# Gathering the U rows and the V rows of 512 tokens apart, with TensorE summing four tokens' V rows in 32-column parts

## The chip, the core and the metric

The kernel runs on one core of one Trainium2 chip. The metric is the device time of one execution in microseconds. The engines are TensorE (PE), VectorE (DVE), ScalarE (ACT), GpSimd (POOL) and SyncE (SP), and 16 DMA engines move data between memory and the on-chip buffers.

## What is computed

Two transformer blocks over 512 tokens of 1024 values in float32: projections, attentions, a convolution, cross attentions, and in the first block a product-key layer with 16384 single-neuron experts. This last part is what the change touches:

```python
# hf: normed tokens, in chunks of 128; 8 heads, 16 experts per head
experts = ...                      # 128 indices per token, from two top-16 lists per head
g = softmax(top_s)
ue = peer_u[experts]               # per token 128 rows of 1024 floats
ve = peer_v[experts]               # per token 128 rows of 1024 floats
act = gelu(einsum('td,thkd->thk', hc, ue))
y = einsum('thk,thkd->td', g * act, ve)
x = x + y
```

That is 512 x 128 rows of U and as many of V, 4 KB each: 537 MB in all.

## The kernel before

The tokens lie in X as four tiles of 128 (partition = token). Tiles 0 and 1 are half 0, tiles 2 and 3 half 1. The program is a list of steps made by `Plan.steps` (from line 454): the first part runs half 0 through the first block (`first_a`), the last part runs half 1 through the second block (`second(1, False)`), and between them three step streams are woven by made-up costs (`weave`, line 85): `work` (half 1 through the first block, then half 0 through the second), `peers` (the experts of all four tiles) and `choices` (the top-16 lists, `choose`). Every engine then runs those steps of the list that concern it, in the order of the list, and waits on semaphores. In `work` nearly every projection is a `proj_T` or `proj_tok` step, planned at 3.4 each, with one 512 KB block of weights that SP loads into RING (6 entries).

An expert step `(t, c)` of `peers` handles the c-th expert of all 128 tokens of tile t, and 512 of them are planned at 3.1 (tiles 0 and 1) or 2.5 (tiles 2 and 3):

- POOL (line 2160) gathers 128 rows of 8 KB from `in_uv`, where the U and the V row of an expert stand side by side, into one of 8 slots of 1 MB in BIG. Partition p gets the row of token p. It waits until the slot's earlier user has been added.
- DVE (line 1943) multiplies the U half by the normed tokens and sums over 1024 values: one dot product per token, in column `k % 8` of `dots`.
- ACT (lines 1441, 1445, 1448) takes the gelu of that one column and scales it by the gate.
- One or two steps later the V half is added to the tokens. For 333 of the experts DVE does it (line 1923, X = V * gate + X). For the other 179 ACT first writes a diagonal matrix of the gates (line 1453), and TensorE multiplies it with the V half into PSUM banks 6 and 7 (lines 1176, 1177). `Plan.peers` picks these 179. After a tile DVE adds the banks to X (`total`, line 1933).

A float32 matmul is recorded as two MATMUL instructions, so an add by TensorE is four of them, of 512 columns each. In the trace, `BIG<-in_uv,BIG` is the gather, `CUSTOM_DVE_ANT_0` of line 1943 the dot product, and `L908`/`L909` the projections of `work`.

## Time and profile before

| | |
|---|---|
| median of 3 runs | 2927.49 us (2926.61 to 2928.93) |
| span of the profiled execution | 2927.4 us |
| own time of the profiled execution | not listed apart from its span; the span is 0.1 us under the median |
| PE busy | 2491.4 us (85%) |
| DVE busy | 1760.7 us (60%) |
| ACT busy | 1133.8 us (39%) |
| POOL busy | 676.9 us (23%) |
| moved by DMA | 838.64 MB, mean 286 GB/s |
| first gather issued, first and last dot product | 559.4 us, 567.2 us and 2306.1 us |

How to read it: busy is the union of an engine's instructions. A stretch is bound by an engine only where that engine's busy time is near the stretch's length, or by the DMA engines where their share is near 1. Half of the kernel's time and more lies between the first and the last expert, so the stretches between them are read one by one, 64 expert steps in each.

### The profile page before, as it was taken

Reading aid. Unit: us, or ns where it says so; the run is one execution under the profiler, and the core shown is the slowest. Engines: PE = TensorE matmul, PEld = TensorE weight load, DVE = VectorE, ACT = ScalarE, POOL = GpSimd, SP = SyncE. Lnnn points to the kernel's source line nnn. Section 1 sums busy time; section 2 is a strip of 40 time slices with the busy share of each in tenths; the row PEclk is TensorE's granted clock in tenths of the full one; section 3 lists DMA queues with packets and bytes.
Section 4 is the critical chain, followed back from the end, with each engine's and each line's share of the span. In section 5 each row is a group of like instructions: output and inputs, shape, how many; then the busy total and the mean of one; then the engine's idle time right before and its main releaser. Section 6 shows DMA issues by size and latency. Waiting matters only on the chain.

```text
span 2927.4 us, 29566 instructions
## 1 busy us (share of the span) xinstructions
PE 2491.4 (85%) x10118; PEld 1743.2 (60%) x10118; DVE 1760.7 (60%) x4222; ACT 1133.8 (39%) x2762; POOL 676.9 (23%) x566
## 2 busy tenths in 40 slices
PE   8999999879989759888968678588985799988998
PEld 7786666667755437546736544264763376655883
DVE  2101311598797778666989888878998416412430
ACT  2101301242533765354442578464554325512210
POOL 0000000122234343332223445444223101100000
PEclk9999999989989889999989578799997999999999
DMA  5545243689999999999899989999999743432443
GB/s 197 173 154 168 95 144 129 219 335 351 390 394 417 409 397 392 419 389 384 299 332 402 365 301 385 396 420 419 417 418 416 277 159 109 151 130 88 153 155 116
DMA packets 160966, 838.64 MB, mean 286 GB/s; under 512 B 17400, under 2 KB 21896, under 8 KB 95024
## 3 DMA queue, kind: packets, MB, share of 16 engines
q0 software_dynamic: 73728, 536.90, 45.8%
q1 hardware_dynamic: 82464, 287.75, 28.0%
q10 hardware_dynamic: 4624, 12.11, 1.1%
q8 instruction: 80, 1.31, 0.2%
q14 instruction: 70, 0.57, 0.1%
HBM read 828.27 MB, written 8.41 MB: 286 GB/s over the span
## 4 chain that ended last, share of the span: by engine, by line
PE 55%; DVE 18%; ACT 12%; DMA 11%; issue 4%; POOL 0%; ACTq 0%; DVEq 0%; SPq 0%
PE ps L908 26%; DMA BIG<-in_uv,BIG 10%; PE ps L928 5%; PE ps L929 5%; PE ps L1152 5%; DVE BIG L1943 5%; DVE X L1923 4%; PE ps L909 4%; PE ps L1176 2%; PE ps L1177 2%; ACT L1441 2%; DVE BIG L1854 1%; PE ps L1122 1%; DVE BIG L1851 1%; PE ps L1101 1%
## 5 line engine op out<-in xcount | busy, mean ns | idle before, releaser
L2160 POOL DMA_INDIRECT BIG<-in_uv,BIG x512 | 634.2, 1239 | 1646.3 <-DVE BIG L1900 564.6
L908 PE MATMUL ps<-BIG,RING 128*128 128x256 f32 x3472 | 807.6, 385 | 13.8 <-DMA RING<-in_w_cq 4.9
L908 PEld LDWEIGHTS ps<-BIG,RING 128*128 128x128 f32 x3472 | 670.1, 194 | 133.4 <-issue 28.6
L1943 DVE CUSTOM_DVE_ANT_0 BIG<-BIG 128x1024 f32<-128x1024 f32 x512 | 619.6, 1217 | 85.4 <-DMA BIG<-in_uv,BIG 84.2
L1923 DVE SCALAR_TENSOR_TENSOR X<-BIG,small,X 128x1024 f32<-128x1024 f32 x333 | 426.6, 1281 | 91.7 <-ACT small L1445 91.6
L1441 ACT ACTIVATE small<-small 128x1 f32<-128x1 f32 x512 | 102.6, 200 | 620.7 <-DVE small L1943 619.4
L908 PE MATMUL ps<-WK,RING 128*128 128x256 f32 x1232 | 287.2, 385 | 25.2 <-DVE BIG L1702 23.2
L908 PEld LDWEIGHTS ps<-WK,RING 128*128 128x128 f32 x1232 | 235.7, 193 | 65.3 <-DVE BIG L1702 31.1
L928 PE MATMUL ps<-RING,BIG 128*128 128x512 f32 (+1 forms) x448 | 223.0, 579 | 5.0 <-DVE BIG L1681 2.4
L929 PE MATMUL ps<-RING,BIG 128*128 128x512 f32 (+1 forms) x448 | 222.6, 578 | 0.0
L1274 ACT ACTIVATE BIG<-ps 128x256 f32<-128x256 f32 (+2 forms) x143 | 56.8, 398 | 408.5 <-PE ps L909 343.2
L1640 DVE TENSOR_SCALAR BIG<-ps 128x256 f32<-128x256 f32 (+2 forms) x37 | 16.8, 454 | 255.8 <-PE ps L909 211.4
L1176 PE MATMUL ps<-BIG,DG 128*128 128x512 f32 x180 | 111.4, 704 | 66.8 <-ACT DG L1453 66.7
L1152 PE MATMUL ps<-RING,BIG 128*128 128x512 f32 x352 | 159.8, 608 | 1.5 <-DVE X L1933 1.5
L896 PE MATMUL ps<-ident,BIG 128*128 128x128 f32 x128 | 47.8, 386 | 131.0 <-ACT BIG L1245 76.2
L1441 ACT ACT_TABLE_LOAD x117 | 150.1, 1283 | 2.7 <-issue 0.6
L909 PE MATMUL ps<-BIG,RING 128*128 128x256 f32 x496 | 147.5, 379 | 0.0
L1633 DVE TENSOR_TENSOR X<-ps,X 128x512 f32<-128x512 f32 x40 | 27.5, 690 | 196.9 <-PE ps L929 116.5
L929 PEld LDWEIGHTS ps<-RING,BIG 128*128 128x128 f32 x448 | 85.1, 190 | 101.0 <-issue 99.5
L928 PEld LDWEIGHTS ps<-RING,BIG 128*128 128x128 f32 x448 | 84.4, 190 | 102.0 <-issue 92.6
L1176 PE MATMUL ps<-BIG 128*128 128x512 f32 x178 | 109.1, 699 | 37.3 <-ACT BIG L1453 37.1
L1223 ACT ACTIVATE WK<-X 128x1024 f32<-128x1024 f32 x32 | 33.8, 1055 | 222.2 <-DVE X L1633 207.2
(259 smaller groups left out, 3136.7 us busy)
## 6 DMA issues: line engine op xcount, KB each, us to landing
RING<-in_w_up SPq DMA_DIRECT2D x88, 512.0 KB, 6.0
RING<-in_w_down SPq DMA_DIRECT2D x66, 512.0 KB, 3.6
RING<-in_w_pq SPq DMA_DIRECT2D x32, 512.0 KB, 6.1
RING<-in_w_cc SPq DMA_DIRECT2D x16, 512.0 KB, 8.1
RING<-in_w_cx SPq DMA_DIRECT2D x16, 512.0 KB, 4.1
RING<-in_w_cb SPq DMA_DIRECT2D x16, 512.0 KB, 4.4
RING<-in_w_cv SPq DMA_DIRECT2D x16, 512.0 KB, 5.0
RING<-in_w_gc SPq DMA_DIRECT2D x16, 512.0 KB, 4.7
```

The costliest lines, as they stand in the source:

```text
L908: e.matmul(ps[:, 0:256], W[:, j, :], src[:, j, 0:256], start=j == 0, stop=False)
L909: e.matmul(ps[:, 0:256], W[:, 7, :], src[:, 7, 0:256], start=False, stop=True).then_inc(pe.sem, pe("mm", site, h, c, m))
L928: e.matmul(ps[:, 0:n], src[:, 2 * j, t * 128:(t + 1) * 128], W[:, 0, :], start=j == 0, stop=False)
L929: mm = e.matmul(ps[:, 0:n], src[:, 2 * j + 1, t * 128:(t + 1) * 128], W[:, 1, :], start=False, stop=j == 3)
L1152: mm = e.matmul(ps[:, :], AF[h][:, f, t * 128:(t + 1) * 128], W[:, hh * 512:(hh + 1) * 512], start=f == 0, stop=f == 21)
L1176: e.matmul(banks[6][:, :], d, v[:, 0:512], start=first, stop=last)
L1177: e.matmul(banks[7][:, :], d, v[:, 512:1024], start=first, stop=last).then_inc(pacc.sem, pacc("sum", k))
L1274: e.activation(dst, ps[:, 0:dst.shape[-1]], ACT.Copy, scale=scale).then_inc(act.sem, act("ev", site, h, c, m))
L1441: e.activation(a, dots[:, k % 8:k % 8 + 1], ACT.Gelu).then_inc(act.sem, act("gelu", k))
L1923: e.scalar_tensor_tensor(out=X[:, t, :], in0=slot[slot_of[k]][:, 1024:2048], scalar=acts[:, k % 8:k % 8 + 1], in1=X[:, t, :], op0=ALU.mult ...
L1943: e.tensor_tensor_reduce(out=u, in0=HF[:, t % 2, :], in1=u, scale=1.0, scalar=0.0, op0=ALU.mult, op1=ALU.add, accum_out=dots[:, k % 8:k % ...
L2160: e.indirect_dma_start(out=slot[i], out_offset=None, in_=I["uv"], in_offset=bass.IndirectOffsetOnAxis(ap=IDX[:, t, c:c + 1], axis=0)).then ...
```

## The change

U and V become two tensors. A step of `peers` is now a row step of 512 KB, U or V, and there are 1024 of them, planned at half of the former cost. The slots are 15 of 512 KB (13 while half 1's score lists borrow two). A V row step exists once all 128 U rows of its tile are in the plan, and goes ahead of any U row step; so the order is U of tile 0, V of tile 0, U of tile 1, and so on.

- U row step `(t, c)`: gather of the c-th expert's U rows for 128 tokens, then DVE's dot product into column c of `DOTS`, which also frees the slot.
- After the 128th U row of a tile: one gelu over 128x128 on ACT, one multiply with the gates on DVE, one transpose by TensorE and a copy (`GATES_T`: partition = expert, column = token). The indices are transposed in the same way after row 104.
- V row step `(t, n)`: gather of the 128 V rows of one token n, partition = expert.
- For every four tokens m, 32+m, 64+m, 96+m: DVE copies 4 gate columns into `SPREAD`, a buffer of zeros, and TensorE does 8 matmuls of a 128x32 stationary part with 512 columns, each into the 32 PSUM partitions that hold its token. All 32 such groups of a tile add up in banks 6 and 7.

DVE's 333 adds, ACT's 512 gelus and 512 scalings, its 179 diagonals and TensorE's 716 MATMUL records for the diagonals go. 512 further gathers, 128 groups of 8 matmuls (16 records each), 128 small copies and 4 chains of gelu, multiply, transpose and copy come. `second(0)` also waits in the plan for the total of tile 1.

```diff
     def take_slot(self, row):
+        lent = self.lent_from is not None and (3, 3) not in self.chosen
+        self.turn += 1
+        if self.turn >= (13 if lent else 15):
+            self.turn = 0
+        self.slot_of[row] = self.turn
...
+            u_ok = u < 512 and (tu, cu // 32) in self.chosen
+            v_ok = v < 512 and tv in summable
+            pace = 1.55 if min(tu, tv) < 2 else 1.25
+            if u_ok and not v_ok:
...
+                yield 0, "urow", tu, cu
+                if cu == 104:
+                    after(0, "turn_ids", tu)
+                if cu == 127:
+                    summable.add(tu)
+                    after(2, "gelu", tu)
+                    after(3, "weigh", tu)
+                    after(4, "turn_gates", tu)
+                yield pace, "pace"
+            elif v_ok:
...
+                yield 0, "vrow", tv, 32 * j + m
+                if j == 3:
+                    after(2, "spread", tv, m)
+                    after(3, "vsum", tv, m)
+                if iv == 127:
+                    after(7, "total", tv)
+                yield pace, "pace"
...
-        NS = 8
+        NS = 15
...
+            def vsum(t, m):
...
+                w.wait_ge(*at["spread", t, m])
+                for j in range(4):
+                    w.wait_ge(*at["slot", "v", t, 32 * j + m])
+                for hh in range(2):
+                    for j in range(4):
+                        d = spread_at(t, m) + 32 * j - m
+                        v = slot[slot_of["v", t, 32 * j + m]][:, hh * 512:(hh + 1) * 512]
+                        mm = e.matmul(banks[6 + hh][32 * j:32 * j + 32, :], SPREAD[:, d:d + 32], v, start=m == 0, stop=m == 31)
+                mm.then_inc(vsums.sem, vsums("vsum", t, m))
...
-                e.scalar_tensor_tensor(out=X[:, t, :], in0=slot[slot_of[k]][:, 1024:2048], scalar=acts[:, k % 8:k % 8 + 1],
-                                       in1=X[:, t, :], op0=ALU.mult, op1=ALU.add).then_inc(acc.sem, acc("sum", k))
...
+            def gelu(t):
+                w.wait_ge(*at["dot", t, 127])
+                e.activation(DOTS[t % 2], DOTS[t % 2], ACT.Gelu).then_inc(act.sem, act("gelu", t))
...
+            def urow(t, c):
+                u = slot[slot_of["u", t, c]]
+                e.tensor_tensor_reduce(out=u, in0=HF[:, t % 2, :], in1=u, scale=1.0, scalar=0.0, op0=ALU.mult,
+                                       op1=ALU.add, accum_out=DOTS[t % 2][:, c:c + 1]).then_inc(dot.sem, dot("dot", t, c))
...
+            def spread(t, m):
+                e.tensor_copy(SPREAD[:, d:d + 97:32], GATES_T[:, m:m + 97:32]).then_inc(dve.sem, dve("spread", t, m))
...
+            def vrow(t, n):
+                i = take(("v", t, n))
+                w.wait_ge(*at["ev", "ids", t])
+                e.indirect_dma_start(out=slot[i], out_offset=None, in_=I["v"],
+                                     in_offset=bass.IndirectOffsetOnAxis(ap=IDX_T[t % 2][:, n:n + 1], axis=0)).then_inc(
+                    slot_in[i].sem, slot_in[i]("slot", "v", t, n))
```

TensorE's order in a part where adds used to stand between the projections of half 1's mixer (L908 and L909 projections, L1176 and L1177 the add of one expert):

```order
L1176 MATMUL ps<-BIG,DG 128x512
L1177 MATMUL ps<-BIG,DG 128x512
L908 MATMUL ps<-BIG,RING 128x256 x7
L909 MATMUL ps<-BIG,RING 128x256
L908 MATMUL ps<-BIG,RING 128x256 x7
L909 MATMUL ps<-BIG,RING 128x256
L1176 MATMUL ps<-BIG,DG 128x512
L1177 MATMUL ps<-BIG,DG 128x512
```

And after the change, where the U rows of tile 0 end (L916 and L917 are the same projections, L1180 the transpose of the gates, L1196 the groups of 8):

```order
L916 MATMUL ps<-BIG,RING 128x256 x7
L917 MATMUL ps<-BIG,RING 128x256
L1180 MATMUL ps<-ident,BIG 128x128
L1196 MATMUL ps<-BIG 32x512 x40
L916 MATMUL ps<-BIG,RING 128x256 x7
L917 MATMUL ps<-BIG,RING 128x256
L1196 MATMUL ps<-BIG 32x512 x8
L916 MATMUL ps<-BIG,RING 128x256 x7
L917 MATMUL ps<-BIG,RING 128x256
L916 MATMUL ps<-BIG,RING 128x256 x7
L917 MATMUL ps<-BIG,RING 128x256
L1196 MATMUL ps<-BIG 32x512 x8
```

Ahead of L1180 no expert work stands on TensorE; behind it a group of 8 follows about every two projections, after a first run of five groups.

DVE's order in tile 0, between the lists of tile 1 (L1943 the dot product, L1923 the add):

```order
L1943 ISA BIG,small<-BIG 128x1024
L1943 ISA small 128x1
L1923 SCALAR_TENSOR_TENSOR X<-BIG,small,X 128x1024
L1851 MAX BIG<-BIG 128x8 x2
L1854 MAX_INDEX BIG<-BIG 128x8 x2
L1859 MATCH_REPLACE BIG<-BIG 128x256 x2
L1851 MAX BIG<-BIG 128x8 x2
L1854 MAX_INDEX BIG<-BIG 128x8 x2
L1943 ISA BIG,small<-BIG 128x1024
L1943 ISA small 128x1
```

And after (L1932 is the dot product, L1858 to L1866 the same lists):

```order
L1932 ISA BIG<-BIG 128x1024
L1932 ISA BIG 128x1
L1932 ISA BIG<-BIG 128x1024
L1932 ISA BIG 128x1
L1932 ISA BIG<-BIG 128x1024
L1932 ISA BIG 128x1
L1858 MAX BIG<-BIG 128x8 x2
L1861 MAX_INDEX BIG<-BIG 128x8 x2
L1866 MATCH_REPLACE BIG<-BIG 128x128 x2
```

The adds are gone, and the dot products stand twice as close.

POOL's order and waits at the border between the U and the V rows of tile 0, after the change (before, every gather of 128x2048 waited for one add):

```order
L2181 DMA BIG<-in_u,BIG 128x1024 [waits expert_dot] x31
L2188 DMA BIG<-in_v,BIG 128x1024 [waits dve_result,expert_dot]
L2188 DMA BIG<-in_v,BIG 128x1024 [waits expert_dot] x14
L2188 DMA BIG<-in_v,BIG 128x1024 [waits expert_rows_summed]
L2188 DMA BIG<-in_v,BIG 128x1024 x3
```

A gather now waits for a dot product 15 rows back, or, every fourth, for a group of four tokens.

## Rows read from the trace of the kernel before

**Rows 1.** The page's 40 slices of the span: DMA share in tenths.

```profile
DMA  5545243689999999999899989999999743432443
```

**Rows 2.** Eight stretches: window and length, busy us (count) of PE, PEld, DVE, ACT, POOL; clock, DMA, GB/s.

```profile
567.20:832.40 265.20, 243.26 (x999) 190.15 (x998) 223.57 (x629) 108.29 (x260) 65.63 (x62) 0.95 0.95 362
832.40:1021.40 189.00, 152.91 (x522) 87.72 (x521) 151.38 (x284) 96.50 (x251) 78.79 (x65) 0.89 1.01 415
1021.40:1240.40 219.00, 170.00 (x662) 120.19 (x661) 169.25 (x261) 106.04 (x250) 90.02 (x66) 0.90 0.98 402
1240.40:1504.10 263.70, 232.88 (x822) 151.22 (x821) 201.70 (x542) 121.41 (x295) 73.27 (x64) 0.96 0.92 357
1504.10:1728.80 224.70, 147.94 (x934) 107.95 (x935) 206.57 (x516) 109.25 (x279) 78.75 (x62) 0.74 0.90 355
1728.80:1916.60 187.80, 137.53 (x450) 77.20 (x449) 167.93 (x424) 123.50 (x343) 97.20 (x65) 0.83 0.96 381
1916.60:2116.90 200.30, 170.94 (x665) 124.41 (x664) 169.11 (x274) 110.23 (x256) 80.69 (x65) 0.96 1.02 418
2116.90:2308.10 191.20, 128.07 (x424) 84.36 (x422) 163.26 (x269) 91.67 (x215) 63.92 (x57) 0.87 0.99 406
```

**Rows 3.** The page's groups: line, engine, op, count, busy us, mean ns, idle before.

```profile
L2160 POOL DMA_INDIRECT BIG<-in_uv,BIG x512 | 634.2, 1239 | 1646.3 <-DVE BIG L1900 564.6
L1923 DVE SCALAR_TENSOR_TENSOR X<-BIG,small,X 128x1024 f32<-128x1024 f32 x333 | 426.6, 1281 | 91.7 <-ACT small L1445 91.6
```

**Rows 4.** DVE busy us of line 1923 alone in the four odd stretches.

```profile
567.20:832.40 265.20, 40.97 (x32) 0.95 0.95 362
1021.40:1240.40 219.00, 65.35 (x51) 0.90 0.98 402
1504.10:1728.80 224.70, 62.76 (x49) 0.74 0.90 355
1916.60:2116.90 200.30, 66.67 (x53) 0.96 1.02 418
```

**Rows 5.** PE busy us of lines 1176 and then 1177, in even stretches: the fourth, and all four.

```profile
1240.40:1504.10 263.70, 37.88 (x70) 12.92 (x70) 0.96 0.92 357
sum 831.70, PE 134.48 PEld 41.83; mean PE 33.62 PEld 10.46
...
1240.40:1504.10 263.70, 36.42 (x70) 13.74 (x70) 0.96 0.92 357
sum 831.70, PE 125.57 PEld 46.85; mean PE 31.39 PEld 11.71
```

**Rows 6.** Timeline of PE at 1000 us: start, length, line, shapes, count.

```profile
1000.21 0.71 PE L951 MATMUL ps<-BIG 64*128 64x256 f32 x4
1000.74 0.60 PE L952 MATMUL ps<-BIG 64*128 64x256 f32 x4
...
1003.96 1.02 PE L1176 MATMUL ps<-BIG 128*128 128x512 f32 x2
1004.82 1.02 PE L1177 MATMUL ps<-BIG 128*128 128x512 f32 x2
```

**Rows 7.** Timeline of DVE from 1744 us, and of POOL from 1743 us.

```profile
1744.58 1.27 DVE L1923 SCALAR_TENSOR_TENSOR X<-BIG,small,X 128x1024 f32<-128x1024 f32 x1
1745.78 1.21 DVE L1943 CUSTOM_DVE_ANT_0 BIG<-BIG 128x1024 f32<-128x1024 f32 x1
1746.92 1.21 DVE L1943 CUSTOM_DVE_ANT_0 BIG<-BIG 128x1024 f32<-128x1024 f32 x1
...
1743.31 5.64 POOL L2160 DMA_INDIRECT BIG<-in_uv,BIG  x1 [0.30 <-issue]
1750.51 0.94 POOL L2160 DMA_INDIRECT BIG<-in_uv,BIG  x1 [0.31 <-issue]
```

**Rows 8.** DMA queues from 2000 to 2190 us: packets, MB, share of 16 engines.

```profile
q0 software_dynamic: 7800, 56.83, 72.0%
q1 hardware_dynamic: 6153, 22.39, 29.5%
```

More of the change, by code:

```diff
@@ L107, in __init__ @@
         self.ring = 0
-        self.light = False
-        self.norming = False
-        self.pe_sums = {t: [] for t in range(4)}
         self.chosen = set()
-        self.slot_of, self.slot_before = [], []
+        self.turn = -1
+        self.free = set()
+        self.slot_of, self.slot_before = {}, {}
         self.last_in = {}
@@ L279, in lists @@
                     yield 0, "trans", ("mem", 2), i, lean
+            while h and not self.free.issuperset(self.lent_from):
+                yield "wait"
             for t in range(2):
@@ L365, in second @@
                  16: ("conv_out", h, 0), 17: ("conv_out", h, 1), 18: ("y_sq", h, 1), 19: ("y_sq", h, 2)}
[L366 to L371 removed]
+        for i in range(20):
+            yield 8.0, "nsa", h, i
+            if i in other:
+                yield (0,) + other[i]
+            yield from beside(1 + i % 2)
         yield 0, "mark", ("y", h)
@@ L442, in peers, with after @@
     def peers(self):
-        late, n = [], 0
-        for t in range(4):
-            for c in range(128):
-                while (t, c // 32) not in self.chosen:
-                    yield "wait"
-                if t == 2 and c == 0:
+        later, n, u, v, rows_first = [], 0, 0, 0, True
+        summable = set()
+        def after(gap, *step):
+            later.append((n + gap, step))
+            later.sort(key=lambda x: x[0])
+        while u < 512 or v < 512 or later:
+            while later and later[0][0] <= n:
+                step = later.pop(0)[1]
+                yield (0,) + step
+                self.reached.add(step)
+                if step[0] == "vsum":
+                    self.free.update(("v", step[1], 32 * j + step[2]) for j in range(4))
+            tu, cu = u // 128, u % 128
+            tv, iv = v // 128, v % 128
+            u_ok = u < 512 and (tu, cu // 32) in self.chosen
+            v_ok = v < 512 and tv in summable
+            pace = 1.55 if min(tu, tv) < 2 else 1.25
+            if u_ok and not v_ok:
+                if tu == 2 and cu == 0:
@@ L531, in half @@
             return X[:, 2 * h:2 * h + 2, :]
[L533 removed]
+        slot = [BIG[:, SLOT0 + 1024 * i:SLOT0 + 1024 * (i + 1)] for i in range(NS)]
         LROW = WK[:, 7, 0:256]
@@ L1938, in expert @@
-            def expert(t, c):
-                k = 128 * t + c
-                u = slot[slot_of[k]][:, 0:1024]
+            def total(t):
+                w.wait_ge(*at["ev", "co", t // 2, 1, 1])
+                w.wait_ge(*at["vsum", t, 31])
+                for hh in range(2):
+                    d = X[:, t, hh * 512:(hh + 1) * 512]
+                    e.tensor_tensor(d, banks[6 + hh][:, :], d, ALU.add).then_inc(dve.sem, dve("total", t))
+                    at["ev", "experts", 6 + hh] = (dve.sem, dve.n)
@@ L2146, in out_T, with take @@
                     e.tensor_tensor(AF[h][:, f, :], AF[h][:, f, :], UPT[f % 4], ALU.mult).then_inc(pool.sem, pool("upm", h, f))
-            def expert(t, c):
-                k = 128 * t + c
-                i = slot_of[k]
-                w.wait_ge(*at["idx", t, c // 32])
-                if slot_before[k] is not None:
-                    w.wait_ge(*at["sum", slot_before[k]])
-                    if i == NS - 1 and slot_before[k] == plan.lent_from:
+            def take(row):
+                i, before = slot_of[row], slot_before[row]
+                if before is not None:
+                    w.wait_ge(*released(before))
+                    if plan.lent_from and before in plan.lent_from:
                         w.wait_ge(*at["idx", 3, 3])
```

219 lines of the change are left out of this document (87 added, 132 removed).

## The prediction

> **What bounds the kernel now.** I read the page's slices first. From the eighth to the 32nd of 73 us each the DMA engines are at 6 to 9 tenths, elsewhere at 2 to 5 [rows 1]. That is the part with the experts, from 559 us to 2308 us. Outside it nothing is changed, so the 567.2 us ahead of the first dot product and the 619.3 us behind 2308.1 are carried over. Then I cut the middle, 1740.9 us, into eight stretches of 64 expert steps [rows 2]. The change gives the first, third, fifth and seventh stretch the U rows of tiles 0 to 3 (U0 to U3), and the even ones the V rows (V0 to V3), because 128 half steps are planned at the cost of 64 whole ones. In rows 2 the reader is to compare a stretch's length with each engine's busy time and with GB/s. 418 GB/s is the most that any stretch shows, with a DMA share of 1.02. A stretch's bytes at 418 GB/s, which is its length times its GB/s over 418, is the least that DMA lets it take: U0 229.7, V0 187.6, U1 210.6, V1 225.2, U2 190.8, V2 171.2, U3 200.3, V3 185.7 us, 1601 in all. So four stretches (V0, U1, U3, V3) stand within 4% of their DMA time. The other four lose 124 us against it, because other engines are near their limit there: in U0 PE is busy 243 and DVE 224 of 265, in V1 PE 233 of 264, in U2 DVE 207 of 225.
>
> A change of 0.2% (5.9 us) is about what a measurement of this kernel can tell from none.
>
> **TensorE.** The adds on it go. They were 260.1 us of busy time in the four even stretches, 74.3 of them in V1 [rows 5], which leaves PE 391.3 and 158.6 us of other work. What comes are 32 groups per V stretch, each of 8 matmuls, 16 records of 512 columns. A record of 512 columns takes 0.43 us: two of line 1176 start 0.86 ahead of the next two [rows 6]. The trace has no matmul with 32 columns in the stationary part. The bounds are: all 16 one after another, 6.9 us; four parts side by side, 16 x 0.43 / 4 = 1.7 us. I take the second with 0.2 us of filling, 1.9 us, 61 us per V stretch, since the nearest row shows parts of the array at work side by side: lines 951 and 952 use 64 rows each in two groups, and four records of 256 columns need 0.53 us to the start of the next four [rows 6], where one after another would be 0.86. Those are groups of rows, the new ones are groups of columns, so the other end stays in the range. The Trainium skill's page "TensorE: Matmul & The Clock Gate", section "Part 3: Packing small matmuls — row/col tiling", gives 2.38 times the speed for three column parts. By that four parts give about 3.2 times, an estimate, and a group would be 2.2 instead of 1.9 us, 10 us more per V stretch; no row here has column parts to agree or not.
>
> **VectorE.** Its 333 adds of 1.28 us go [rows 3]. The dot products stay, but all of them now stand in the U stretches: 64 more in each than before. Back to back a dot product costs 1.14 us (1745.78 to 1746.92), and an add 1.20 [rows 7]. So a U stretch has its busy time [rows 2], less its adds [rows 4], plus 73.4 us: U0 223.6 - 41.0 + 73.4 = 256, U1 177, U2 217, U3 176 us. In U0 this is 26 us above the DMA time, in U2 as well. The V stretches lose 73 us of dot products and their adds, and get 32 copies of 4 columns, at nothing: the longest V stretch keeps DVE under 100 of 264 us. The gain there is hidden, since DVE did not set the end of V0 and V3, and DMA takes its place.
>
> **ScalarE.** 1024 short instructions and 179 diagonals go, and four gelus over 128x128 come. ACT was busy at most 123 us of 188 [rows 2], so this saves only what waited for it, and I count it in the idle time of V1 and V2. What the four chains at the borders cost (last dot product, gelu, multiply, transpose, copy, first group) is some 5 us each; DMA works on through them, since up to 15 V rows may be under way, so they cost nothing but in U0 and U2, where DVE is the limit; it is in the idle time that I leave there.
>
> **DMA.** The bytes are the same, in 4 KB pieces instead of 8 KB. From 2000 to 2190 us, with the engines full, the gathers took 72.0% of 16 x 190 us for 56.83 MB, 38.5 us per MB, and the weights, in pieces of 4 KB, 29.5% for 22.39 MB, 40.1 us per MB [rows 8]. The gathers will be like the second: 67.1 MB x 1.54 / 16 = 6.5 us more per stretch. The bounds are 0 and this.
>
> **GpSimd.** 512 gathers more. A free one takes 0.94 us and 0.30 of issue [rows 7], 1.25 us per row, 160 us per stretch: under the DMA time everywhere. But the mean is 1.24 us instead of 0.94 [rows 3]. The long ones are those that start while DVE runs a dot product or an add: the one at 1743.31 took 5.64 us, through a dot product, an add and two more dot products without a gap [rows 7]. In a U stretch a dot product (1.14 us) comes with every row. If a gather starts at any time, it meets one with the chance 1.14 / T and waits 0.57 us on average, T being the time per row: T = 1.25 + 0.65 / T, T = 1.62 us, 208 us per stretch. That is as much as DMA needs in U1 (217) and U3 (207). Two queues of the same speed with 15 slots between them lose some time against either; I take 11 to 13 us.
>
> **The sum**, in us: U0, DVE 256 and about half of the 42 idle of before, 275 (before 265.2). V0, DMA 187.6 + 6.5 and 2, 196 (189.0). U1, 217 + 11, 228 (219.0). V1, DMA 231.7, PE 158.6 + 61 = 220, both near, and 13 of the 31 us that PE stood idle, 245 (263.7). U2, DVE 217 and the 18 of idle time of before, 236 (224.7). V2, 177.7 + 4, 182 (187.8). U3, 206.8 + 13, 220 (200.3). V3, 192.2 + 5, for the last group and the last total, 197 (191.2). Together 1779 instead of 1740.9, and with 567.2 and 619.3 around them 2965 us. The profiled span, 2927.4, stands 0.1 us from the median of the runs, so nothing is added. The two gains (V1, V2: 25 us) are smaller than what six stretches lose (63 us). Work is not cut where DMA is the limit, and the dot products of two stretches are pushed into one.
>
> **The rivals.**
>
> 1. Faster: the stretches run at their limits, without a charge for small pieces and without gathers that wait for DVE. DMA would set V0 188, U1 211, V1 with some idle time of PE 232, V2 172, U3 200, V3 186, DVE with a few us each U0 266 and U2 225: 1680 us, 2866 in all. For it speaks that PE, DVE and ACT all have more room in the V stretches than they ever had; against it the mean of the gathers [rows 3] and the two prices per MB [rows 8]. A half of it, 2915, is as likely as the whole.
>
> 2. The change doesn't do on TensorE what it says: the 32-column parts run one after another, at 7 us per group with filling. 391.3 + 128 x 7 = 1287 us of PE in the V stretches, every one of them bound by it, against 820 in my sum: 3432 us. If two of four run side by side, a group is 3.6 us, 115 per V stretch. V1 then has PE 274 instead of 245, and V3 in its first half, where the projections of line 908 stand, some 25 more: about 3025 us.
>
> 3. Slower through GpSimd: with rows that have landed waiting in the slots, DVE runs dot products without a gap, and no gather gets in until it runs dry. Its point is where rows land faster than 1.14 us plus DVE's other work per row. If each gather waited out one whole dot product, a row would be 1.14 + 1.25 = 2.4 us, 306 per U stretch, 1224 instead of 959: 3230 us. Against it: with an empty queue DVE has gaps, so it mends itself. The Trainium skill's page "SBUF — State Buffer", section "SBUF: two separate sides", calls the ports that VectorE and GpSimd share an exclusive lock, held for a whole instruction; with two SBUF inputs on VectorE it names as blocked only GpSimd work that reads SBUF. By the lock alone this rival holds in full; the row of 5.64 us agrees with the lock, the rows of 0.94 say that a gather that has begun is not held up.
>
> **Chances.** My forecast, a modest loss from full DMA queues, DVE and GpSimd in the U stretches, 0.55, mostly between 2934 and 3000. Rival 1 and its half 0.27. Rival 2 in full 0.05, in half 0.07. Rival 3 in full 0.06. Faster by over 0.2%: 0.30, rival 1 and a small part of the forecast's own spread. Within 0.2%, between the forecast and the half of rival 1: 0.12. Slower: 0.58. The range leaves out rivals 2 and 3 in full, which is 0.11, and some 0.06 below; it reaches from 2868, where rival 1 ends, to 3045, a little over the half of rival 2.
>
> **What would show it.** A group of L1196 every 1.9 us where its rows are there, DMA share near 1 in V0, U1, U3 and V3; DVE busy for over nine tenths of U0 and U2, under four tenths of the V stretches; more idle time on PE at the end of U0 (PE waiting for the copy of GATES_T); POOL busy about 1100 us or more, with a mean above 1.2 us in U rows and 0.94 to 1.0 in V rows; weights and gathers at the same 40 us per MB. I am wrong if U0 and U2 are not longer than before, if the V stretches beat 418 GB/s, or if a group takes 3.6 or 7 us.

## The result, and the profile after

The changed kernel takes 2947.49 us (median of 4 runs, 2942.99 to 2951.17) against 2928.21 (4 runs, 2926.61 to 2932.33): ratio 1.0068, 95% interval 1.0051 to 1.0084. It is slower by 0.7%. The profiled execution took 2942.99 us, its span is 2940.8 us. The forecast was 2965 us.

The page's groups that answer to [rows 3] (line, engine, op, count, busy us, mean ns, idle before and what ended it): L2181 gathers U, L2188 gathers V, L1932 is the dot product, L1196 the groups of four tokens.

```profile
L2181 POOL DMA_INDIRECT BIG<-in_u,BIG x512 | 665.3, 1299 | 797.1 <-DVE BIG L1907 556.6
L1932 DVE CUSTOM_DVE_ANT_0 BIG<-BIG 128x1024 f32<-128x1024 f32 x512 | 607.9, 1219 | 113.2 <-DMA BIG<-in_u,BIG 111.4
L2188 POOL DMA_INDIRECT BIG<-in_v,BIG x512 | 507.2, 991 | 336.3 <-PE ps L1196 186.2
L1196 PE MATMUL ps<-BIG 128*32 128x512 f32 x2048 | 282.1, 675 | 99.4 <-DMA BIG<-in_v,BIG 83.5
```

A gather of U rows, beside which dot products run, takes 1.30 us in the mean, one of V rows 0.99. The eight stretches, with the columns of [rows 2], are U0, V0, U1, V1, U2, V2, U3, V3 from top to bottom:

```profile
564.30:836.00 271.70, 203.89 (x926) 176.57 (x924) 257.07 (x726) 35.31 (x77) 171.80 (x138) 0.90 0.96 364
836.00:1025.10 189.10, 154.18 (x880) 72.87 (x880) 39.97 (x155) 30.48 (x76) 119.19 (x126) 0.89 1.01 398
1025.10:1258.60 233.50, 152.46 (x618) 117.25 (x618) 183.44 (x339) 34.58 (x75) 173.90 (x133) 0.81 0.98 381
1258.60:1501.50 242.90, 231.11 (x1169) 133.54 (x1169) 95.49 (x416) 49.34 (x110) 114.92 (x119) 0.96 0.98 372
1501.50:1731.90 230.40, 115.95 (x892) 94.51 (x884) 218.32 (x573) 44.85 (x105) 180.03 (x129) 0.66 0.94 354
1731.90:1908.40 176.50, 138.44 (x810) 63.79 (x811) 58.25 (x319) 57.13 (x178) 124.91 (x131) 0.89 1.02 401
1908.40:2126.70 218.30, 160.34 (x593) 116.83 (x593) 178.79 (x341) 35.88 (x81) 170.74 (x130) 0.80 0.99 382
2126.70:2329.80 203.10, 168.68 (x945) 97.71 (x945) 41.45 (x142) 23.55 (x45) 113.62 (x120) 0.92 1.00 400
```

Against [rows 2], U0 to U3 are longer by 6.5, 14.5, 5.7 and 18.0 us, V1 and V2 shorter by 20.8 and 11.3, V0 the same, V3 longer by 11.9. Together 1765.5 instead of 1740.9. Ahead of the first dot product it is 564.3 us instead of 567.2, behind the last stretch 611.0 instead of 619.3. Of these 8.3 us, 3.9 come from where I cut: of the kernel before the last `total` lies behind my cut and begins 3.9 us after it, of the kernel after the cut is at that `total`. I did not follow the other 4.4; the 2916 us kernel below has 618.4 us behind its last `total`, where this one has 611.0.

The reader is to see three things in the rows. No stretch goes over 401 GB/s, where [rows 2] had 415 and 418. DVE (the third pair) is at 257 of 272 and 218 of 230 us in U0 and U2. And in the V stretches DVE is busy for only 20 to 39% of the time and ACT for 12 to 32%, and still only V1 and V2 became shorter. The granted clock is lower than before in U1 and U3 (0.81 and 0.80 instead of 0.90 and 0.96), but PE is busy for 152 of 234 and 160 of 218 us there, so it does not set their length.

The DMA queues from 2250 to 2320 us, in V3, where the engines are full (packets, MB, share of 16 engines; q0 are the gathers):

```profile
q0 software_dynamic: 7280, 26.52, 95.0%
```

0.950 x 16 x 70 us over 26.52 MB is 40.1 us per MB, the price of the weights in [rows 8], where gathers of 8 KB cost 38.5. The rate there is 409 GB/s.

PE's timeline in V0 (start, length, line, shapes, records):

```profile
870.76 0.59 PE L917 MATMUL ps<-BIG,RING 128*128 128x256 f32 x2
871.29 1.92 PE L1196 MATMUL ps<-BIG 128*32 128x512 f32 x16
873.14 3.29 PE L916 MATMUL ps<-BIG,RING 128*128 128x256 f32 x14
```

A group of 16 records, 1.92 us, between two projections: the forecast's 1.9. Of the 128 groups, 111 begin while the granted clock is at its upper level (2.4 GHz), with a median of 1.92 us; the 17 at the lower level (1.2 GHz) have 3.37. PE's busy time by the groups alone, in V1:

```profile
1258.60:1501.50 242.90, 61.71 (x496) 13.64 (x496) 0.96 0.98 372
```

That is the 61 us of the forecast, with a clock of 0.96. In the other V stretches it is 69 to 71 us, with clocks of 0.89 to 0.92.

POOL's and DVE's timelines at 1042 us, in U1, where dot products stand back to back:

```profile
1041.00 0.94 POOL L2181 DMA_INDIRECT BIG<-in_u,BIG  x1 [0.30 <-issue]
1042.24 1.56 POOL L2181 DMA_INDIRECT BIG<-in_u,BIG  x1 [0.30 <-issue]
1044.11 1.99 POOL L2181 DMA_INDIRECT BIG<-in_u,BIG  x1 [0.30 <-issue]
```

```profile
1041.77 1.22 DVE L1932 CUSTOM_DVE_ANT_0 BIG<-BIG 128x1024 f32<-128x1024 f32 x1
1042.92 1.22 DVE L1932 CUSTOM_DVE_ANT_0 BIG<-BIG 128x1024 f32<-128x1024 f32 x1
1044.06 1.22 DVE L1932 CUSTOM_DVE_ANT_0 BIG<-BIG 128x1024 f32<-128x1024 f32 x1
```

The gather of 1041.00, which begins before the dot products, takes 0.94 us; the next two begin while they run and take 1.56 and 1.99. None waits for a slot ("issue" only). Of the 512 gathers of U rows, 275 begin while DVE is in an instruction of over 1 us, and take 1.57 us in the mean; the other 237 take 0.99.

### The profile page after: what moved, and what is told of

Same layout as the page of the kernel before. It is cut to its first block, busy times and chain, and to the rows that moved or that the text cites. A ratio compares the mean times of both kernels' runs of the same rounds, so it can differ in the third digit from the quotient of the medians.

```text
span 2940.8 us, 30892 instructions
## 1 busy us (share of the span) xinstructions
PE 2423.2 (82%) x11458; PEld 1667.8 (57%) x11458; DVE 1380.2 (47%) x4033; ACT 577.6 (20%) x1363; POOL 1215.6 (41%) x1079
## 4 chain that ended last, share of the span: by engine, by line
PE 29%; POOL 9%; DVE 7%; DMA 3%; issue 3%; ACT 1%; ACTq 0%; DVEq 0%
PE ps L916 11%; POOL BIG L2181 6%; PE ps L1160 5%; DVE BIG L1932 3%; PE ps L1196 3%; POOL BIG L2188 3%; DMA BIG<-in_v,BIG 2%; PE ps L936 2%; PE ps L937 2%; PE ps L917 2%; DMA BIG<-in_u,BIG 1%; PE ps L1130 1%; PE ps L1109 1%; ACT WK L1243 0%; PE ps L1061 0%
## 5 line engine op out<-in xcount | busy, mean ns | idle before, releaser
L2181 POOL DMA_INDIRECT BIG<-in_u,BIG x512 | 665.3, 1299 | 797.1 <-DVE BIG L1907 556.6
L916 PE MATMUL ps<-BIG,RING 128*128 128x256 f32 x3472 | 811.6, 386 | 40.6 <-DVE BIG L1676 20.7
L916 PEld LDWEIGHTS ps<-BIG,RING 128*128 128x128 f32 x3472 | 668.7, 194 | 159.1 <-issue 23.1
L1932 DVE CUSTOM_DVE_ANT_0 BIG<-BIG 128x1024 f32<-128x1024 f32 x512 | 607.9, 1219 | 113.2 <-DMA BIG<-in_u,BIG 111.4
L2188 POOL DMA_INDIRECT BIG<-in_v,BIG x512 | 507.2, 991 | 336.3 <-PE ps L1196 186.2
L1196 PE MATMUL ps<-BIG 128*32 128x512 f32 x2048 | 282.1, 675 | 99.4 <-DMA BIG<-in_v,BIG 83.5
L916 PE MATMUL ps<-WK,RING 128*128 128x256 f32 x1232 | 288.5, 387 | 1.5 <-DVE WK L1629 0.8
L916 PEld LDWEIGHTS ps<-WK,RING 128*128 128x128 f32 x1232 | 236.8, 194 | 49.8 <-issue 15.1
L936 PE MATMUL ps<-RING,BIG 128*128 128x512 f32 (+1 forms) x448 | 227.8, 590 | 9.3 <-DVE BIG L1688 5.0
L937 PE MATMUL ps<-RING,BIG 128*128 128x512 f32 (+1 forms) x448 | 224.2, 582 | 0.0
L1196 PEld LDWEIGHTS ps<-BIG 128*32 128x32 f32 x2048 | 62.1, 117 | 259.1 <-issue 214.6
L936 PEld LDWEIGHTS ps<-RING,BIG 128*128 128x128 f32 x448 | 83.7, 192 | 113.8 <-issue 100.2
L917 PE MATMUL ps<-BIG,RING 128*128 128x256 f32 x496 | 147.5, 379 | 0.0
L937 PEld LDWEIGHTS ps<-RING,BIG 128*128 128x128 f32 x448 | 85.9, 192 | 102.6 <-issue 101.2
L2164 POOL TENSOR_TENSOR BIG<-BIG,WK 128x256 f32<-128x256 f32 x22 | 15.9, 725 | 295.0 <-DVE WK L1706 295.0
L1160 PEld LDWEIGHTS ps<-RING,BIG 128*128 128x128 f32 x352 | 65.7, 191 | 77.4 <-issue 76.4
```

The source lines that it names most:

```text
L916: e.matmul(ps[:, 0:256], W[:, j, :], src[:, j, 0:256], start=j == 0, stop=False)
L917: e.matmul(ps[:, 0:256], W[:, 7, :], src[:, 7, 0:256], start=False, stop=True).then_inc(pe.sem, pe("mm", site, h, c, m))
L936: e.matmul(ps[:, 0:n], src[:, 2 * j, t * 128:(t + 1) * 128], W[:, 0, :], start=j == 0, stop=False)
L937: mm = e.matmul(ps[:, 0:n], src[:, 2 * j + 1, t * 128:(t + 1) * 128], W[:, 1, :], start=False, stop=j == 3)
L1160: mm = e.matmul(ps[:, :], AF[h][:, f, t * 128:(t + 1) * 128], W[:, hh * 512:(hh + 1) * 512], start=f == 0, stop=f == 21)
L1196: mm = e.matmul(banks[6 + hh][32 * j:32 * j + 32, :], SPREAD[:, d:d + 32], v, start=m == 0, stop=m == 31)
```

## The experiments

Four questions: do the parts stand side by side on TensorE because their columns differ; what do the smaller gathers cost alone; is it VectorE that makes the U gathers long; and would another order of the rows, or of the work beside them, be better.

The first seven runs were made on one chip, four of the last five on a second and one on a third; for the runs of the result the chip is not on record. The section on the last five says why this may matter.

### The four tokens of a group in the same columns

```diff
...
-                        mm = e.matmul(banks[6 + hh][32 * j:32 * j + 32, :], SPREAD[:, d:d + 32], v, start=m == 0, stop=m == 31)
+                        q = m // 8
+                        mm = e.matmul(banks[6 + hh][32 * q:32 * q + 32, :], SPREAD[:, d:d + 32], v, start=m % 8 == 0 and j == 0,
+                                      stop=m % 8 == 7 and j == 3)
...
```

> Against the kernel after, the four tokens of a group lie in the same 32 columns (tokens 4m to 4m+3) instead of in four different ones; the instructions have the same shapes and count. Theory A (the four parts work side by side only since they are different columns): a group of 16 records goes from 1.92 us to about 6.9 us, TensorE has some 880 us instead of 282 in groups, and the time goes to about 3400 us. Theory B (a part of 32 columns is cheap by itself, whichever it is): a group stays near 2 us, the time near 2947.

Measured: 3441.03 us, one run. The same number and size of matmuls, four tokens now in one 32-column part; the order of the V rows and the copies into `SPREAD` follow it. The page's group and a row of PE's timeline, a group of four (L1197 is the line of the groups here):

```profile
L1197 PE MATMUL ps<-BIG 128*32 128x512 f32 x2048 | 902.3, 598 | 6.5 <-DVE BIG L1963 6.5
```

```profile
879.51 7.05 PE L1197 MATMUL ps<-BIG 128*32 128x512 f32 x16
```

A group takes 7.05 instead of 1.92 us, and the kernel 494 us more. Thus the four parts run side by side, 3.7 times as fast, when they lie in different columns and so in different PSUM partitions; the run does not tell these two apart. The prediction's second rival had 7 us per group and 3432 us; its price was right, its condition does not hold. The Trainium skill, "TensorE: Matmul & The Clock Gate", "Part 3: Packing small matmuls — row/col tiling", gives 2.38 for three column parts, by which I had worked out 3.2 and 2.2 us as an estimate. With four parts the trace shows more than that.

### The kernel before, with each gather in two of 4 KB

```diff
-                e.indirect_dma_start(out=slot[i], out_offset=None, in_=I["uv"],
+                e.indirect_dma_start(out=slot[i][:, 0:1024], out_offset=None, in_=I["u"],
...
+                e.indirect_dma_start(out=slot[i][:, 1024:2048], out_offset=None, in_=I["v"],
```

> The kernel before, with its order, its 8 slots and its adds, but each 8 KB gather issued as two of 4 KB, U and V. It isolates the price of 1024 gathers in small pieces. Theory A (4 KB pieces cost 6.5 us per stretch where DMA is full, and GpSimd's 1.25 us per gather plus its waits for VectorE come to 3 us per expert and more, which is what the fastest stretches have): 2970 to 3000 us. Theory B (both are hidden, and the kernel after lost its time only by its order): 2928 to 2935 us.

Measured: 2985.81 us (2983.50 to 2988.78), ratio 1.0212 (1.0195 to 1.0229). Groups of its page, and the queue of its gathers from 2000 to 2190 us, the window of [rows 8]:

```profile
L2160 POOL DMA_INDIRECT BIG<-in_u,BIG x512 | 596.7, 1165 | 987.4 <-DVE BIG L1900 562.2
L2163 POOL DMA_INDIRECT BIG<-in_v,BIG x512 | 600.7, 1173 | 156.6 <-issue 156.6
```

```profile
q0 software_dynamic: 16138, 58.76, 78.4%
```

The gathers now cost 0.784 x 16 x 190 / 58.76 = 40.6 us per MB. My price of 6.5 us per stretch was 52 us in eight, and this kernel lost 59. Which part of it is the size of the pieces and which the 512 further issues on GpSimd, this run does not separate. It does say that the rest of the change (order, slots of half the size, the new sums) is worth about 38 us: it brings this kernel's 2985.8 to 2947.5. The time is inside the 2970 to 3000 us of theory A.

### The tokens of tiles 1 to 3 read from PSUM

Banks 6 and 7 are free from one `total` to the first group of the next tile. ScalarE copies the normed tokens there, and from row 16 on, the dot products of tiles 1 to 3 read them there; only the gathered row comes from SBUF. Tile 0 is left as it was.

```diff
+            def hf_copy(t):
+                w.wait_ge(*at["hf", t // 2, 1])
+                w.wait_ge(*at["total", t - 1])
+                e.activation(ps67[:, 0:512], HF[:, t % 2, 0:512], ACT.Copy, scale=1.0).then_inc(act.sem, act("hfc", t))
+                e.activation(ps67[:, 512:1024], HF[:, t % 2, 512:1024], ACT.Copy, scale=1.0).then_inc(act.sem, act("hfc", t))
...
+                h = HF[:, t % 2, :]
+                if t and c > 15:
+                    w.wait_ge(*at["hfc", t])
+                    h = ps67[:, :]
```

> Against the kernel after, ScalarE copies the normed tokens of tiles 1 to 3 into PSUM banks 6 and 7 once their last use by the tile before is over, and the dot products from row 16 on read them from there, so that they have one input in SBUF instead of two. Theory A (the gathers of U rows are late because a dot product with two inputs in SBUF holds a port that GpSimd needs): U row gathers of tiles 1 to 3 fall from a mean of 1.30 to 1.34 us to under 1.05 us, their stretches from 233.5, 230.4 and 218.3 us to about 222, 222 and 209, and the time by 20 to 30 us, to about 2922 us. Theory B (DMA sets U1 and U3, VectorE U2, and the gathers have slack): the gathers may get shorter, the time stays within 5 us of 2947. Theory C (it is not the port): the gathers stay at 1.30 us.

Measured: **2916.25 us** (6 runs, 2913.54 to 2922.54), ratio 0.9968 (0.9955 to 0.9980) to the kernel before. It beats both kernels, the kernel before by a third of a per cent. POOL's busy time (count) by the U gathers alone, with clock, DMA share and GB/s behind it, in U0 to U3, first of the changed kernel:

```profile
564.30:836.00 271.70, 154.08 (x125) 0.90 0.96 364
1025.10:1258.60 233.50, 160.58 (x119) 0.81 0.98 381
1501.50:1731.90 230.40, 167.31 (x124) 0.66 0.94 354
1908.40:2126.70 218.30, 159.68 (x121) 0.80 0.99 382
```

and of this one (L2195 is the same gather):

```profile
561.50:830.10 268.60, 153.00 (x125) 0.89 0.97 368
1020.50:1243.40 222.90, 117.67 (x119) 0.80 1.01 398
1485.10:1713.50 228.40, 123.14 (x123) 0.65 0.97 375
1887.10:2097.70 210.60, 118.62 (x121) 0.83 1.00 398
```

The mean of a gather falls from 1.35, 1.35 and 1.32 to 0.99, 1.00 and 0.98 us in U1 to U3, and stays at 1.23 and 1.22 in U0, where nothing was changed. The dot product itself takes as long as before:

```profile
L1946 DVE CUSTOM_DVE_ANT_0 BIG<-ps,BIG 128x1024 f32<-128x1024 f32 x336 | 395.2, 1217 | 43.6 <-DMA BIG<-in_u,BIG 42.6
L1946 DVE CUSTOM_DVE_ANT_0 BIG<-BIG 128x1024 f32<-128x1024 f32 x176 | 209.6, 1218 | 45.7 <-DMA BIG<-in_u,BIG 45.4
```

So the long gathers come from VectorE reading two operands in SBUF, and go when one of them is in PSUM. Which step of a gather is held up, the trace does not show. POOL is busy with these gathers for 536.5 us instead of 665.3, and the kernel takes 31 us less. In U1 and U3 the rate rises from 381 and 382 to 398 GB/s, near the 409 of full queues, and they are 10.6 and 7.7 us shorter. U2 stays bound by DVE and gives 2 us, where theory A had 8.

This comparison needs care, since the chip of the changed kernel's runs is not on record. Up to the first dot product of tile 1 the two kernels do the same work, and the two traces agree to 2 us: U0 and V0 together are 460.8 us in the changed kernel and 459.0 here. The two traced executions differ by 20 us, not 31, as the one here is the slowest of six and the other the fastest of four; U1 to U3 are 20.3 us of the difference.

### U and V rows in turn

One row of U, one of V, as soon as a tile's V rows can go; and the same by fours.

```diff
-            if u_ok and not v_ok:
+            if u_ok and (rows_first or not v_ok):
```

> Only the order of the row steps is changed against the kernel after: where both kinds are to be had, a V row and a U row take turns, instead of V rows always ahead. Theory A (the U stretches are held by VectorE's dot products and by GpSimd's gathers that wait for them, the V stretches have room on both): with the dot products of tiles 1 to 3 spread over both kinds of stretches only the U rows of tile 0 stay dense, the mean gather falls from 1.15 us (1.30 for U rows, 0.99 for V rows) to about 1.1, and the time to about 2890 us. Theory B (from the first gather to the last the DMA engines set the time, whose small pieces cost the same in any order): 2935 to 2950 us, as after (2947.5).

```diff
-            if u_ok and not v_ok:
+            if u_ok and (not v_ok or (v % 4 == 0 and (u % 4 or rows_first))):
```

> The kernel of e1_alternate (3070 us), but four U rows and four V rows in turn instead of one and one. In e1 VectorE waited 510 us for U rows to land and TensorE 229 us for copies that stand behind those dot products. Theory A (a group's four V rows are held over eight row steps while they wait for each other, and hold back the 15 slots and POOL's queue behind them): the time falls well under 3070, to between 2960 and 3020 us. Theory B (it is that the copies for TensorE stand in VectorE's queue behind dot products whose rows have not landed, in whichever order): 3050 to 3100 us again.

Measured: 3069.9 us (3062.76 to 3072.52), ratio 1.0488 (1.0470 to 1.0505), and by fours 2975.62 (2963.59 to 2979.70), ratio 1.0168 (1.0139 to 1.0196). The first missed both times that I had written, the second is in the range of its theory A. Waits from 560 to 2400 us (engine, line, releaser: us in total, times, longest), row by row:

```profile
DVE BIG L1932 <- DMA BIG<-in_u,BIG: 509.9, 266, 9.6
POOL BIG L2181 <- PE ps L1196: 284.1, 63, 15.1
PE ps L1196 <- DVE BIG L1961: 228.8, 47, 13.3
```

and by fours:

```profile
DVE BIG L1932 <- DMA BIG<-in_u,BIG: 381.6, 159, 12.4
PE ps L1196 <- DVE BIG L1961: 226.3, 45, 10.9
POOL BIG L2181 <- PE ps L1196: 191.4, 45, 16.3
```

I read these rows as three queues in a ring. With both kinds under way, a U gather waits for slots that V rows hold, a V row holds its slot until its group of four is summed, and the group waits for a copy that stands in DVE's queue behind dot products, which wait for U rows. DVE stood 510 us for rows to land, against 111 in the changed kernel. By fours, 94 of the 122 us that turns cost are back. PE's wait for the copies stayed (229 and 226 us); what fell is GpSimd's wait for slots and DVE's for rows, as it would if groups that wait for their rows held fewer slots. That this is the reason is my reading; no run varies the slots alone on this chip. From tile 1 on, the dot products are spread over the time in both kernels, and it does not pay for these waits. Rows of one kind at a time, as in the change, are the better order with 15 slots.

### The lists of the next tile in the V stretches

DVE is busy 257 of 272 us in U0, with 128 dot products and the lists of tile 1, and 40 of 189 in V0. So the lists of tiles 1 and 3 were held back until the indices of the tile ahead are transposed, after its row 104, and every list is planned at a cost of 1, so that they come faster from there on.

```diff
-                while ("sc", t // 2, p) not in self.reached:
+                while ("sc", t // 2, p) not in self.reached or (t % 2 and ("turn_ids", t - 1) not in self.reached):
...
-                yield from self.choose(t, p, (1.0, 3.0, 1.0, 2.0)[t])
+                yield from self.choose(t, p, 1.0)
```

> Against the kernel after, the top-16 lists of tiles 1 and 3 are chosen later and faster: not beside the U rows of tiles 0 and 2, but from row 104 of these on, so that most of them falls beside the V rows. Theory A (U0 and U2 are held by VectorE, whose lists and dot products meet there, as predicted): U0 goes from 272 to some 235 us and U2 from 230 to some 210, and of these 55 us most stays as gain, since V0 and V2 have VectorE free: 2895 to 2915 us. Theory B (U0 and U2 are held by GpSimd's gathers, 1.6 to 1.7 us per row whatever VectorE does beside the dot products, or by DMA at 236 and 203 us): U0 stays above 255, the gain is under 15 us, 2932 to 2947.

> The kernel of e2_tokens_from_psum (2916 us) with the lists moved as in e5_lists_in_v. If VectorE's load in U0 and U2 and the gathers' waits in U1, U2 and U3 are separate losses, their gains add up: 2916 less what e5 gains against 2947.5, so 2870 to 2890 us by theory A. If the two are one loss, it stays at 2905 to 2916.

Measured: alone 3008.81 us (3008.23 to 3013.49), ratio 1.0294 (1.0277 to 1.0311); with the tokens in PSUM 2985.24 (2979.68 to 2986.12), ratio 1.0203 (1.0186 to 1.0220). Neither time is in a range that I had written. With the lists moved, the tokens in PSUM are still worth 24 us. The first of the two kernels from 1650 to 1830 us, columns as in [rows 2]:

```profile
1650.00:1830.00 180.00, 63.75 (x386) 39.74 (x390) 169.08 (x631) 36.97 (x123) 87.91 (x78) 0.55 0.71 253
```

Cut as above, U0 is 268.5 us, only 3 less, V0 grew from 189 to 206.5, and U2 from 230.4 to 251.4: DVE is at 169 of 180 us in the window shown, and DMA at 0.71. The lists do hold U0 up. Its first 96 dot products, now without lists beside them, took 189.1 us from the first to the start of the 97th, instead of 213.0. But the rest of U0, with all the lists beside it, took 79 us instead of 59. The work was moved to where it costs as much or more. A second effect is mixed in: two slots are lent until the last list of tile 3 is chosen, so a later list means 13 slots for longer.

### Five runs on other chips

> The kernel of e2_tokens_from_psum (2916 us) with the lists of tiles 1 and 3 started only when the gates of the tile before have been turned, so wholly beside V rows; in e5 they stood from row 104 on and made the last 24 U rows take 78 instead of 58 us. Theory A (U0 is held by VectorE): row 96 of tile 0 lands as early as in e5 (750 instead of 777 us) and U0 ends by 805 us instead of 836; the projections of k then wait some 30 us for the lists, which V0 hides in part: 2885 to 2900 us. Theory B (what U0 gives is taken again by the projections that wait): 2910 to 2935 us.

> As e2_tokens_from_psum, with only tile 3's lists moved, to behind tile 2's gates. Theory A (U2 is held by VectorE's lists and dot products, as predicted): U2 goes from 233 to about 215 us, 2898 to 2905 us in all. Theory B (in e5 the first 96 U rows of tile 2 took 163 us without lists and 168 with them, so U2 is held by something else, DMA and the steps of the second block): within 5 us of 2916.

> The kernel after, with every dot product over 512 of the 1024 values (half of each sum is left out; the gathers are whole). VectorE then has some 75 us less in each U stretch, and holds its port half as long. Theory A (U stretches are held by VectorE or by gathers that wait for it): U0 from 272 to about 240, U1 from 237 to 222, U2 from 235 to 210, U3 from 225 to 212, 2860 to 2870 us. Theory B (DMA with small pieces holds U1 to U3, VectorE only U0): 2905 to 2920 us.

> The kernel after with 12 slots in turn instead of 15 (10 while two are lent). Theory A (gathers and weights keep the DMA queues full with 8 rows under way, and in the U stretches GpSimd does not wait for slots in 454 of 512 issues): 2950 to 2965 us. Theory B (the number of rows under way sets the rate, which is also why e1 and e7 were slow, where V rows hold their slots longer): over 2980 us.

> The kernel with the tokens in PSUM (2916 us) had U0 268.7, V0 190.3, U1 225.9, V1 238.8, U2 232.7, V2 169.3 us. Here the planned cost of a row differs by stretch: tile 0 U 1.45 and V 1.65, tile 1 U 1.70 and V 1.40, tile 2 U 1.20 and V 1.30, tile 3 1.25. By the plan four of the 55 projections of U0 move to V0, and the first part of V1's other work to U1; nothing is added or taken away. Theory A: a stretch is as long as the work put beside it where an engine is near its limit, and its bytes over 409 GB/s elsewhere, so work moved from U0 and V1 into V0 and U1 is hidden there: U0 some 8 us shorter, V1 some 10, V0 and U1 longer by at most 8 together, 2900 to 2910 us. Theory B: the order in which the engines' queues meet steps of the other stream decides, since a queue that stands at such a step keeps landed rows in their slots: the moved work brings waits of over 6 us on GpSimd (10 in that kernel) to new places, and the time is 2916 us or more.

Their edits, in this order: to the kernel with the tokens in PSUM, lists of tiles 1 and 3 behind `turn_gates` of the tile ahead; only those of tile 3; to the changed kernel, dot products over 512 of the 1024 values (it leaves out the other half of each sum); 12 slots (10 while two are lent); to the kernel with the tokens in PSUM, planned costs by stretch.

```diff
-                while ("sc", t // 2, p) not in self.reached:
+                while ("sc", t // 2, p) not in self.reached or (t % 2 and ("turn_gates", t - 1) not in self.reached):
...
-                while ("sc", t // 2, p) not in self.reached:
+                while ("sc", t // 2, p) not in self.reached or (t == 3 and ("turn_gates", t - 1) not in self.reached):
...
-                e.tensor_tensor_reduce(out=u, in0=HF[:, t % 2, :], in1=u, scale=1.0, scalar=0.0, op0=ALU.mult,
+                e.tensor_tensor_reduce(out=u[:, 0:512], in0=HF[:, t % 2, 0:512], in1=u[:, 0:512], scale=1.0, scalar=0.0, op0=ALU.mult,
...
-            self.turn = 0
+            self.turn = 3
...
-            pace = 1.55 if min(tu, tv) < 2 else 1.25
+            pace = ((1.45, 1.65), (1.70, 1.40), (1.20, 1.30), (1.25, 1.25))[min(tu, tv, 3)][v_ok]
```

| edit | us | ratio to the kernel before |
|---|---|---|
| lists of tiles 1 and 3 behind the gates | 3054.45 | 1.0436 (1.0406 to 1.0466) |
| only tile 3's | 3074.60 | 1.0498 (1.0466 to 1.0529) |
| half dot products | 2984.29 | 1.0182 (1.0137 to 1.0228) |
| 12 slots | 3020.05 | 1.0319 (1.0292 to 1.0345) |
| planned costs by stretch | 3025.06 | 1.0350 (1.0328 to 1.0372) |

All five are slower than I could explain, the one with half the dot products too, whose DVE has some 270 us less to do. The first three are outside every range that I had written. The second gives the reason to distrust the totals. Its program is the same, instruction for instruction on every engine, as that of the 2916 us kernel until late in V1. The transposes of the gates of tile 0 and tile 1 (L1184) on PE, first in the 2916 us kernel:

```profile
831.32 0.45 PE L1184 MATMUL ps<-ident,BIG 128*128 128x128 f32 x1 [7.36 <-DVE BIG L1961]
...
1247.19 0.33 PE L1184 MATMUL ps<-ident,BIG 128*128 128x128 f32 x1 [2.44 <-DVE BIG L1961]
```

and in the run with tile 3's lists moved:

```profile
829.62 0.45 PE L1184 MATMUL ps<-ident,BIG 128*128 128x128 f32 x1 [7.37 <-DVE BIG L1868]
...
1283.98 0.47 PE L1184 MATMUL ps<-ident,BIG 128*128 128x128 f32 x1 [2.44 <-DVE BIG L1961]
```

Equal instructions between the two took 415.9 us in one and 454.4 in the other. So at least 38 of the 158 us between these kernels are no effect of the edit. Each of the two figures is from one execution. PE's timeline in that run shows where some of it goes:

```profile
1136.26 3.19 PE L920 MATMUL ps<-BIG,RING 128*128 128x256 f32 x14
1139.28 0.59 PE L921 MATMUL ps<-BIG,RING 128*128 128x256 f32 x2
...
1145.47 0.58 PE L920 MATMUL ps<-BIG,RING 128*128 128x256 f32 x1 [2.42 <-issue]
...
1149.69 0.58 PE L920 MATMUL ps<-BIG,RING 128*128 128x256 f32 x1 [2.24 <-issue]
1151.80 0.59 PE L920 MATMUL ps<-BIG,RING 128*128 128x256 f32 x1 [1.52 <-issue]
```

A projection whose 16 records take 3.6 us is stretched to some 18, with pauses of up to 2.4 us in which PE waited for nothing that the profile shows. The waits of PE from 560 to 2340 us have such rows in each of the five runs, and none over 0.2 us in the kernel before, the changed one and the seven runs on the first chip. For the run above the row with the largest sum is

```profile
PE ps L920 <- issue: 63.2, 43, 2.4
```

In the other runs single ones are longer, up to 19.7 us with half the dot products. The timeline holds a pattern. Between 1144.07 and 1155.30 us, PE's weight loads and matmuls start about 0.70 us or twice that apart (the matmuls shown: 4.22 and 2.11 us, six and three times 0.70). From 560 to 2340 us, such distances come 27 to 115 times in each of the five runs and at most 5 times in the others. The pauses shown began while the granted clock was at 1.00 (1139 to 1141 us); it fell to its lower level, 1.2 GHz, only at 1143 us.

DVE then waits for that projection with landed rows in the slots, GpSimd waits for the slots (20.7 us before the gather at 1172.21), and the DMA share falls (to 0.50 from 1165 to 1175 us). What holds PE back stays open: the DMA engines are full at the time (401 GB/s from 1130 to 1156 us), as they are in the runs without such pauses. The kernel before, timed beside these runs, had medians of 2924 to 2927 us on all three chips. The changed kernel itself and the 2916 us kernel were not timed on these chips, so it is open whether they keep their times there. The totals of these five runs therefore settle nothing on slots, half dot products, lists or planned costs, though the times of two (12 slots and planned costs) fit a theory B that I had written down.

One stretch can be read all the same. In U0, the runs with the lists moved have no such pause on PE, and that with half dot products has 12 us of them. All three are from the same chip, and in U0 they differ in nothing but this. U0, with the columns of [rows 2], with only tile 3's lists moved (nothing changed in U0), with tile 1's lists moved out of it, and with half dot products:

```profile
560.10:828.40 268.30, 205.87 (x925) 177.63 (x923) 257.04 (x728) 35.23 (x77) 173.76 (x138) 0.89 0.96 368
561.90:814.30 252.40, 203.97 (x925) 177.93 (x924) 213.67 (x512) 33.63 (x73) 177.12 (x139) 0.90 0.99 385
563.70:815.50 251.80, 205.15 (x899) 174.93 (x898) 190.40 (x728) 33.21 (x72) 140.94 (x136) 0.88 0.99 381
```

The first is as long as in the 2916 us kernel on its own chip (268.6). With 43 or 67 us less for DVE, U0 is 16 us shorter. So VectorE bound U0. The DMA share is then 0.99, and I take DMA to be why it is no more than 16 us. What the moved lists cost in V0 and in U2 is not separated from the pauses.

## Why the prediction was right, and where it was off

The forecast was slower, 2965; it is slower, 2947. Step by step:

- **TensorE.** 1.9 us per group forecast, 1.92 measured at the upper clock level. PE busy in V1 was 220 us by the forecast and 231 measured: the groups have their 61 us, and the 11 us more are other work, 169 instead of 158.6.
- **VectorE.** U0 to U3 forecast 256, 177, 217, 176 us busy; measured 257.1, 183.4, 218.3, 178.8. U0 and U2 took 271.7 and 230.4 us where the forecast had 275 and 236. That VectorE binds U0 is shown by the two runs that took work from it; for U2 it rests on its 218 busy us of 230.
- **DMA.** 40.1 us per MB forecast and measured. The run of the kernel before in 4 KB pieces puts it and the further issues at 59 us together, beside my 52 for the pieces alone.
- **GpSimd.** T = 1.62 us per U row forecast; 1.30 and 0.30 of issue are 1.60. The equation of the prediction, solved exactly, gives 1.65 us, 211 us per stretch instead of 208. That fits U1 and U2, where a gather takes 1.35 us. The chance in it was too high (275 of 512 gathers met an instruction of over 1 us, 54%, where 1.14 / T is 70%), and a gather that meets none takes 0.99 us, not 0.94. That the two cancel is luck. That it is VectorE's operands in SBUF is now shown by the PSUM run. Rival 3, a whole dot product waited out each time (2.4 us per row, 3230 us), does not hold: nearly half of the gathers begin outside such an instruction, and those that meet one take 0.58 us more, not 1.14 (the prediction had 0.57). On the page "SBUF — State Buffer" of the Trainium skill, section "SBUF: two separate sides", the lock with two SBUF inputs blocks only GpSimd work that reads SBUF. The runs agree with a lock that goes when an input is in PSUM, and the gather, whose 128 indices are in SBUF, is among the work it holds up.
- **The stretches.** 275, 196, 228, 245, 236, 182, 220, 197 forecast; 271.7, 189.1, 233.5, 242.9, 230.4, 176.5, 218.3, 203.1 measured. The two misses of 7 and 6 us, V0 and V3, are a step that I left out: weights don't stay in their stretch. (U1, U2 and V2 are off by nearly as much, 5.5 us each. The 11 and 13 us that U1 and U3 were to lose to two queues of one speed were a guess; they came out at about 16 and 12.) V0 moved 189.1 x 398 = 75.3 MB instead of 78.4, V3 81.2 instead of 77.6. At 409 GB/s that is 184 and 199 us.
- **The rest.** Of the 24.7 us between 2965.5 and the span of 2940.8, the stretches are 13.5, the part behind them 8.3 and the part ahead 2.9. I carried both outer parts over unchanged.

The first rival, with full DMA speed and no hindered gathers, had a condition that the PSUM run supplies: with the gathers free from U1 on, the change is a gain of 0.3%, at 2916 us, the half of this rival and not the whole. Its other condition, no price for small pieces, does not hold.

## What to carry to other kernels

Splitting one gather into two of half the size costs here twice, 59 us in all in the kernel before: 4% in DMA time per byte, and a second issue of 1.25 us on GpSimd. What it buys has to be counted in the stretches that DMA doesn't bind, and here it showed in two of eight, V1 and V2. Where indirect gathers issued by GpSimd and VectorE run side by side, try one of VectorE's operands in PSUM if a bank is free; here it cost two copies per tile and won 31 us. And before a small difference is explained, compare two kernels over a part in which their instructions are the same: as much as that part differs, the difference is not the edit's.

## What I had not expected

- The price of the new sums came out within 0.02 us: four 32-column parts at 128 rows take 1.92 us for 16 records, against 7.05 in one part, though no row of the kernel before had column parts.
- With the second operand in PSUM the dot product takes the same 1.22 us, and the gathers beside it 0.98 to 1.00 instead of 1.32 to 1.35 us.
- Two kernels that are identical up to late in V1 took 415.9 us for the same stretch on one chip and 454.4 on another, 9% more, with pauses of over 2 us between matmuls of one projection, while the kernel before kept its 2924 to 2927 us on all.
